# Two chained transformer blocks: block 1's first products are taken from the unnormalized x, and their results scaled by a row of inverse norms

## The reference, cut to what matters

```python
def rmsnorm(x, g):
    xf = x.astype(jnp.float32)
    y = xf * lax.rsqrt(jnp.mean(xf * xf, axis=-1, keepdims=True) + EPS)
    return (y * g.astype(jnp.float32)).astype(x.dtype)

def conformer_conv(u, b_glu, w_dw, b_dw, ln_g, ln_b):
    u = u + b_glu
    a, gate = jnp.split(u, 2, axis=-1)
    z = a * jax.nn.sigmoid(gate)
    ...          # causal depthwise convolution of 31 taps, layer norm, silu

def parallel_mixer(h, w_in, ...):        # h = rmsnorm(x, norm_mix_g)
    proj = h @ w_in
    q, k, v = ...                        # 512 columns each
    log_f = jax.nn.log_sigmoid(proj[..., OFF_F:OFF_C] + b_forget)
    attn = forgetting_attention(q, k, v, log_f)
    conv = conformer_conv(proj[..., OFF_C:], ...)
    return jnp.concatenate([attn, conv], axis=-1) @ w_out
```

## Time and profile before

| | us |
|---|---|
| median of the runs | 1259.65 |
| the profiled execution's own time | 1261.36 |
| its span, first to last instruction | 1259.5 |
| PE busy | 1097.0 (87%) |
| DVE busy | 624.7 (50%) |
| ACT busy | 437.5 (35%) |
| chain that ended last: PE / DMA / DVE / ACT | 58% / 32% / 6% / 2% |

### The profile page before, as it was taken

One profiled execution on the slowest core, in us unless ns is written; L12 is line 12 of the kernel. 1 busy time (PEld: TensorE's weight loads), 2 busy tenths in 40 slices (PEclk: granted clock), 3 DMA queues, 4 the chain that ended last, 5 costly groups with the idle time before them and its releaser, 6 DMA issues.

```text
span 1259.5 us, 17506 instructions
## 1 busy us (share of the span) xinstructions
PE 1097.0 (87%) x7555; PEld 792.5 (63%) x7555; DVE 624.7 (50%) x1005; ACT 437.5 (35%) x627; POOL 9.1 (1%) x19
## 2 busy tenths in 40 slices
PE   7999999998665666565768999999999999999997
PEld 6987898743121132121315988888886689998876
DVE  5998845620000000000004698986798766564465
ACT  4245434210000000000004566644586535544353
POOL 0000000000000000000000100000000000000000
PEclk9999999999798788898869999999999999999999
DMA  9543395699999999999999454554544064445430
GB/s 363 201 141 136 148 376 206 229 427 424 426 426 429 426 425 427 427 426 427 426 427 379 156 172 149 170 165 151 200 176 160 39 238 182 159 178 201 167 134 34
DMA packets 30031, 332.29 MB, mean 264 GB/s; under 512 B 3472, under 2 KB 3872, under 8 KB 5760
## 3 DMA queue, kind: packets, MB, share of 16 engines
q1 hardware_dynamic: 28928, 328.11, 66.0%
q0 software_dynamic: 1024, 3.02, 0.7%
HBM read 330.07 MB, written 1.05 MB: 263 GB/s over the span
## 4 chain that ended last, share of the span: by engine, by line
PE 58%; DMA 32%; DVE 6%; ACT 2%; issue 1%; SPq 0%; DVEq 0%; ACTq 0%
PE ps L632 13%; PE ps L649 11%; PE ps L709 10%; DMA arena<-in_w_up 10%; DMA arena<-in_w_down 7%; PE ps L1394 6%; DMA ring<-in_w_gate 4%; DMA arena<-in_w_gate 3%; DMA spare<-in_w_up 3%; DMA ring<-in_w_down 3%; PE ps L847 2%; PE ps L738 2%; PE ps L1026 2%; DMA ring<-in_units 1%; PE ps L761 1%; PE ps L584 1%
## 5 line engine op out<-in xcount | busy, mean ns | idle before, releaser
L1528 DVE TENSOR_TENSOR parts<-ring,parts 128x2048 fp32r<-128x2048 f32 x70 | 160.0, 2291 | 97.5 <-ACT parts L2377 97.0
L2377 ACT CAST parts<-ring 128x2048 fp32r<-128x2048 f32 x70 | 133.1, 1905 | 151.5 <-PE ps L632 66.8
L649 PE MATMUL ps<-parts 128*128 128x512 f32 x768 | 181.5, 394 | 0.9 <-DVE parts L1528 0.9
L1852 DVE TENSOR_TENSOR arena<-arena,ps 128x512 f32<-128x512 f32 x8 | 5.5, 687 | 340.0 <-PE ps L1026 340.0
L649 PEld LDWEIGHTS ps<-parts 128*128 128x128 f32 x768 | 143.1, 189 | 33.0 <-issue 2.8
L632 PE MATMUL ps<-parts 128*128 128x256 f32 x1344 | 163.2, 284 | 0.0
L632 PEld LDWEIGHTS ps<-parts 128*128 128x128 f32 x1344 | 161.9, 192 | 0.2
L709 PE MATMUL ps<-parts 128*128 128x512 f32 x576 | 137.2, 396 | 0.4 <-DVE parts L1697 0.4
L709 PEld LDWEIGHTS ps<-parts 128*128 128x128 f32 x576 | 108.0, 190 | 26.0 <-issue 3.0
L1026 PE MATMUL ps<-ring,arena 128*32 128x512 f32 x528 | 77.6, 721 | 41.8 <-DMA ring<-in_w_up 23.0
L1026 PE MATMUL ps<-arena 128*32 128x512 f32 x400 | 62.5, 760 | 36.2 <-DMA arena<-in_w_up 19.5
(11 more groups left out here) (373 smaller groups left out, 1336.4 us busy)
## 6 DMA issues: line engine op xcount, KB each, us to landing
ring<-in_units SPq DMA_DIRECT2D x35, 2048.0 KB, 8.2
ring<-in_w_gate SPq DMA_DIRECT2D x19, 2048.0 KB, 43.6
ring<-in_units SPq DMA_DIRECT2D x37, 1024.0 KB, 5.3
ring<-in_w_down SPq DMA_DIRECT2D x15, 2048.0 KB, 43.8
ring<-in_w_up SPq DMA_DIRECT2D x14, 2048.0 KB, 43.3
arena<-in_w_up SPq DMA_DIRECT2D x9, 2048.0 KB, 41.8
arena<-in_w_down SPq DMA_DIRECT2D x9, 2048.0 KB, 45.5
arena<-in_w_gate SPq DMA_DIRECT2D x6, 2048.0 KB, 43.5
```

Source lines behind the costliest of these rows:

```text
L649: mm = nc.tensor.matmul(banks[t], v[:, 4 * h + k, t * P:t * P + P], w[:, k, :], start=h + k + n == 0, stop=h == 1 and k == 3 and n == 2)
L1528: step(V.tensor_tensor(rest_half(name, h), split_half(name, h), w_high[stage][h].bitcast(F32), ALU.subtract), f"{stage}_rest_ready", wait= ...
L2377: step(S.copy(w_high[stage][h], split_half(name, h)), f"{stage}_high_ready", wait=False)
```

## The change

PE turns x itself, as soon as it and the identity matrix have landed. The sums of squares, the root and the reciprocal are taken meanwhile. DVE lays the inverse norms on the diagonals of two 128x128 matrices, and PE multiplies these by ones, which gives a row of inverse norms on every partition (`mix_row`). DVE scales by this row: the gates and the values of the convolution, the forget logits, and a whole copy of the turned x (`mix_x`), whose high part and rest then serve `q`, `k` and `v`. The memory's norm on DVE stands no longer ahead of the first gated channels but after the second. SP issues `q` ahead of `conv_a1`, and the memory behind `k`. Banks are dealt from bank 7 on, so that with the one more bank of `mix_row` all later ones get the numbers they had.

```diff
-        used, held, turn = [0] * BANKS, set(), [0]
+        used, held, turn = [0] * BANKS, set(), [7]
...
                 for t in range(TT):
-                    normed_half("mixT", t, t + 1)
-                idle_products(10)
+                    pe.wait_ge(sem(f"x_landed{t}"), 16)
+                    turn_half("mixT", x, t)
+                idle_products(6)
...
+                        if (c, name) == (0, "conv_g"):
+                            pe.wait_ge(sem("mixer_x_made"), 1)
+                            bank = open_bank("mix_row")
+                            for t in range(TT):
+                                mm = nc.tensor.matmul(bank[:, t * P:t * P + P], row_ones, row_diag[:, t * P:t * P + P], start=True, stop=True)
+                            close_bank(mm, "mix_row")
-                pe.wait_ge(sem("mixer_x_rest_ready"), 1)
+                pe.wait_ge(sem("mixer_x_made"), 3)
...
 (DVE)
+                step(V.memset(row_ones, 1.0), wait=False)
+                step(V.memset(z[:, :, 0:TAPS - 1], 0.0), wait=False)
+                step(V.memset(key_bias, 0.0), wait=False)
                 dve.wait_ge(sem("x_landed0"), 16)
-                normalize_half(x, normed, 4, 0)
+                step(V.tensor_tensor_reduce(normed[:, 0, :], x[:, 0, :], x[:, 0, :], 1.0, 0.0, ALU.mult, ALU.add, stat(4, 1)))
+                dve.wait_ge(sem("params_landed"), 16)
+                half_turned("mixT", xT, 0, "norm_mix_g")
+                half_turned("mixT", xT, 1, "norm_mix_g")
                 dve.wait_ge(sem("second_squared"), 1)
-                inverse_rms(stat(5, 1), stat(5, 1), D)
-                step(V.tensor_scalar(normed[:, 1, :], x[:, 1, :], stat(5, 1), None, ALU.mult), "x_normed")
+                inverse_rms(stat(4, 2), stat(4, 2), D)
+                step(V.tensor_scalar(row_diag[:, 0:P], ident, stat(4, 1), None, ALU.mult), wait=False)
+                step(V.tensor_scalar(row_diag[:, P:T], ident, stat(5, 1), None, ALU.mult), "mixer_x_made", wait=False)
...
+                bank = filled_by(dve, "mix_row")
+                drain(V.tensor_copy(mix_row, bank[:, 0:T]), "mix_row", wait=True)
+                def scale_gates(f):
+                    bank = filled_by(dve, f"conv_g{f}")
+                    ins = V.tensor_tensor(glu[:, 2 * f:2 * f + 2, :], grid(bank, 2), wide(mix_row.unsqueeze(1), [P, 2, T]), ALU.mult)
+                    drain(ins, f"conv_g{f}", wait=True)
+                scale_gates(0)
+                step(V.tensor_tensor(mix_x, xT, wide(mix_row.unsqueeze(1), [P, KT, T]), ALU.mult), "mixer_x_made", wait=False)
                 dve.wait_ge(sem("mixer_x_high_ready"), 1)
-                step(V.tensor_tensor(mix_rest, xT, mix_high.bitcast(F32), ALU.subtract), "mixer_x_rest_ready", wait=False)
-                dve.wait_ge(sem("mem_landed"), 16)
-                normalize(mem_tok, mem_normed, 0, "mem_normed")
+                step(V.tensor_tensor(mix_rest, mix_x, mix_high.bitcast(F32), ALU.subtract), "mixer_x_made", wait=False)
...
                 def gated_channels(f):
                     bank = filled_by(dve, f"conv_a{f}")
+                    ins = V.tensor_tensor(z[:, 2 * f:2 * f + 2, TAPS - 1:ZW], grid(bank, 2), wide(mix_row.unsqueeze(1), [P, 2, T]), ALU.mult)
+                    drain(ins, f"conv_a{f}", wait=True)
+                    dve.wait_ge(sem("gate_ready"), f + 1)
...
+                scale_gates(1)
                 convolve(range(1, 11), range(2))
                 gated_channels(1)
+                dve.wait_ge(sem("mem_landed"), 16)
+                normalize(mem_tok, mem_normed, 0, "mem_normed")
                 convolve(range(1, 8), range(2, 4))
                 split_rest("mixer", 1, 0)
...
 (ACT)
-                root()
+                act.wait_ge(sem("params_landed"), 16)
+                half_turned("mixT", xT, 0, "norm_mix_g")
                 act.wait_ge(sem("x_landed1"), 16)
                 step(S.activation(normed[:, 1, :], x[:, 1, :], ACT.Square, accum_out=stat(5, 1)), "second_squared", wait=False)
+                half_turned("mixT", xT, 1, "norm_mix_g")
                 root()
...
 (SP)
                 for c in range(2):
                     for name in BY_COLUMNS:
+                        if (c, name) == (1, "conv_a"):
+                            load(2)
                         load_columns(name, c)
-                sp.dma_start(mem_tok, d["mem"][0].rearrange("(t p) n -> p t n", p=P)).then_inc(sem("mem_landed"), 16)
-                for n in range(2, n_early):
+                for n in range(3, n_early):
                     load(n)
                     if n == 3:
+                        sp.dma_start(mem_tok, d["mem"][0].rearrange("(t p) n -> p t n", p=P)).then_inc(sem("mem_landed"), 16)
```

More of the change, by code:

```diff
@@ L322, in two_blocks_kernel @@
         mix_high, mix_rest = [grid(parts(n), KT) for n in (5, 1)]
+        mix_x = grid(page(1), KT)
+        row_ones, row_diag, mix_row = page(8, 1024, P), page(8, 1152, T), page(8, 1408, T)
         mem_high, mem_rest = [grid(parts_of_page[n][:, :], KT) for n in (8, 9)]
@@ L899, in _ @@
                 split_token_major("mem_kv3", "mem_v1", mem_high, mem_rest, turn_attention)
-                split_token_pair("out", {(1, 1): lambda: normed_half("normT", 0, 3)})
+                split_token_pair("out", {(1, 1): lambda: normed_half("normT", 0, 1)})
                 half_turned("normT", 0)
-                feature_pair(["mem_q0"], xT, lambda: normed_half("normT", 1, 4), lambda: half_turned("normT", 1))
+                feature_pair(["mem_q0"], xT, lambda: normed_half("normT", 1, 2), lambda: half_turned("normT", 1))
                 pe.wait_ge(sem("cross_x_rest_ready"), 1)
@@ L1568, in _ @@
-                dve.wait_ge(sem("mixer_x_high_ready"), 1)
-                step(V.tensor_tensor(mix_rest, xT, mix_high.bitcast(F32), ALU.subtract), "mixer_x_rest_ready", wait=False)
-                dve.wait_ge(sem("mem_landed"), 16)
-                normalize(mem_tok, mem_normed, 0, "mem_normed")
-                step(V.memset(z[:, :, 0:TAPS - 1], 0.0), wait=False)
-                step(V.memset(key_bias, 0.0))
+                inverse_rms(stat(4, 2), stat(4, 2), D)
+                dve.wait_ge(sem("ident_landed"), 16)
@@ L1578, in gated_channels @@
                     for cb in (2 * f, 2 * f + 1):
-                        ins = V.scalar_tensor_tensor(out=z[:, cb, TAPS - 1:ZW], in0=bank[:, (cb % 2) * T:(cb % 2) * T + T],
-                                                     scalar=col("b_glu", cb), in1=glu[:, cb, :], op0=ALU.add, op1=ALU.mult)
-                    drain(ins, f"conv_a{f}", wait=True)
+                        own = z[:, cb, TAPS - 1:ZW]
+                        step(V.scalar_tensor_tensor(out=own, in0=own, scalar=col("b_glu", cb), in1=glu[:, cb, :], op0=ALU.add, op1=ALU.mult),
+                             wait=cb % 2 == 1)
@@ L1613, in _ @@
                 tmp = page(4, 0, 1024)[0:HEADS, :].rearrange("p (n t) -> p n t", n=4)
-                drain(V.tensor_scalar(tmp[:, 0, :], bank[0:HEADS, 0:T], forget_b[:, 0:1], None, ALU.add), "forget", wait=True)
+                drain(V.tensor_tensor(tmp[:, 0, :], bank[0:HEADS, 0:T], mix_row[0:HEADS, :], ALU.mult), "forget", wait=True)
+                step(V.tensor_scalar(tmp[:, 0, :], tmp[:, 0, :], forget_b[:, 0:1], None, ALU.add))
                 step(V.tensor_scalar(tmp[:, 1, :], tmp[:, 0, :], -1.0, None, ALU.mult))
@@ L2077, in _ @@
                     rotate(k_rot, k_rot, NSA_KV)
-                step(V.memset(cmp_hid, 0.0), "cmp_hid_cleared")
+                step(V.memset(cmp_hid, 0.0), "cmp_cleared")
                 for h in range(2):
@@ L2112, in _ @@
                 filled_by(dve, "nq_rotT3")
-                step(V.memset(page(13, 1024, 1024), 0.0), "cmp_v_cleared", wait=False)
+                step(V.memset(page(13, 1024, 1024), 0.0), "cmp_cleared", wait=False)
                 step(V.memset(page(9, 0, 1024), 0.0), wait=False)
@@ L2393, in copy_out @@
                     drain(S.activation(dst, bank, func, scale=scale), fill)
-                root()
+                act.wait_ge(sem("params_landed"), 16)
+                half_turned("mixT", xT, 0, "norm_mix_g")
                 act.wait_ge(sem("x_landed1"), 16)
                 step(S.activation(normed[:, 1, :], x[:, 1, :], ACT.Square, accum_out=stat(5, 1)), "second_squared", wait=False)
+                half_turned("mixT", xT, 1, "norm_mix_g")
                 root()
[L2399 to L2403, removed]
                 def channel_gates(f):
-                    bank = filled_by(act, f"conv_g{f}")
+                    drained_by(act, f"conv_g{f}")
                     for cb in (2 * f, 2 * f + 1):
-                        ins = S.activation(glu[:, cb, :], bank[:, (cb % 2) * T:(cb % 2) * T + T], ACT.Sigmoid, bias=col("b_glu", 4 + cb))
-                    drain(ins, f"conv_g{f}")
+                        ins = S.activation(glu[:, cb, :], glu[:, cb, :], ACT.Sigmoid, bias=col("b_glu", 4 + cb))
```

(9 more changed lines are left out.)

9 lines of the change are left out of this document (3 added, 6 removed).

## The result

The changed kernel takes 1268.88 us (median of four runs, 1266.82 to 1269.97) against 1259.68 (1259.02 to 1260.97): 1.0065 times as long, interval 1.005 to 1.0081. Forecast were 1268.5. The profiled execution took 1268.83 us, with a span of 1267.1 (1259.5 before). Three executions further down, of 1435.87, 1586.5 and (kernel before) 1585.68 us, ran at mean granted clocks of 0.74, 0.65 and 0.65, and all medians and ratios here leave them out.

A forecast was written before the change was run, and what follows sets the result against it. PE alone was taken to bound the old chain from 7.42 to 62.7 us. Start 0.4, mix_row 0.45, wait for k's rest 5.9 and clock 2.1 gave 8.85, so 1259.65 + 8.85 = 1268.5 us; range 1264.5 to 1272.

The forecast's parts named there:

- The wait in front of k: PE, between q and k: DVE has the first rest of k at 57.8, PE wants it at 52.0; 5.9 us.
- The clock behind it: PE at k's start: slow clock after standing still for 5.9 us; 2.1 us lost, with 0 and 2.7 as ends.
- mix_row: PE, ahead of q: two added full products of 128 columns on its path, 0.22 us each, 0.45 together.
- The start: PE's first full unit at about 12.3 instead of 11.88, behind ACT's table load and copies; 0.4 us later.
- The slow first unit: Rival: PE starts conv_g0 at 1.2 GHz after a short wait, some 2 us lost, 1270.5 us; chance 0.15.
- What follows: After block 1's start, through the experts: PE leads, no later cover, so its shift counts at full size, 8.8 us.
- Loads and bank numbers: Earlier q, later conv_a1 and memory, new bank numbers and a joined semaphore: claimed to cost nothing.

The follow-up runs named there:

- a variant: Changed kernel with one small activation ahead of everything on ACT, so that its table is loaded at the start; 1268.36 us, ratio 1.0056.
- Filling the gap: Changed kernel with 44 idle products on PE between q and k, timed twice; 1268.2 us (ratio 1.007) and 1266.16 us (1.0058).
- both repeats: The changed kernel timed and profiled again twice, unchanged; 1268.69 and 1268.2 us, ratio 1.0068 each against the kernel before.
- the four variants without a gap there: Changed kernel with 20 idle products instead of 6 (1267.76 us), table load plus 44 idle products (1265.8), early table load alone (1268.36), or four cures together (1259.9).
- the second repeat: The changed kernel, unchanged, as yardstick of a later group and third look at its first unit; 1268.2 us, ratio 1.0068.

## Why the prediction was right

The path was right: the written order of DVE's line, with the memory's norm in it, makes PE wait in front of `k`, and the slow clock follows. The total lies within half a microsecond of the forecast of 1268.5 partly by luck: a term of 1.9 us that I had left out of the sum was made up for by one that was too large and by what got lost on the way to the end.

**The wait in front of k** was forecast at 5.9 us and measured at 5.87, 5.81 and 5.81. Its working held link by link: 7.7 us from `mix_row` to the first gated channels (21.24 to 28.89, 7.65), 30.3 from there to the rest (28.89 to 59.16, 30.27). Both ends came 1.4 us later than written, with the slow first unit in front of them. Moving the norm (4.7 us) in either kernel, either way, made and unmade the wait as the sum says: 4.7 less of it in the changed kernel, 2.99 us where there had been none in the old one.

**The clock behind it:** 2.1 forecast; 1.9, 1.9 and 1.7 measured in the three profiles of the changed kernel, and 0.2 of restart; 2.5 in a variant. Filling the gap took the clock's part away.

**mix_row:** 0.45 and 0.46.

**The start** was mis-sized: 12.3 forecast, 11.92 measured, +0.04 for +0.4. Two things were off by little: the identity matrix landed 0.1 us earlier and PE began at 6.01, and I had laid ACT's steps end to end, while the square begins 1.02 us behind the start of four copies that are written down with 1.14. That the load stands behind the bank, the step that undid the 1.2 us of earlier transposes, was right (7.21), and taking it away gave 1.3 us.

**The slow first unit** was a rival with a chance of 0.15, and it came true in all three profiles of the changed kernel: 1.9 us. I weighed it by a gap of 1.61 us in the experts that left the clock up. PE here had only just begun to work, and slowly: its 16 transposes took 3.4 to 3.7 us, where 32 took 3.84 at 2.4 GHz. That this is the difference is argued and not shown, since the same start also gave fast units. With this term the kernel should have been at 1259.65 + 10.2, near 1270; the runs say 1268.9. So the total was hit with a term too few in it, and about one microsecond that did not arrive.

**What follows:** that the shift goes on whole is right up to the experts (10.2 at 240 us, 10.6 at 299). At the end it is between 7.6 and 8.7 us in three profiles (spans of 1267.1, 1268.2 and 1267.9 against 1259.5). Of the first pair's difference 1.7 us is the clock in the second block; the rest goes in small steps, half a microsecond in the experts (9.7 behind the last of them, 10.0 in both repeats) and 0.7 up to 965 us (1.1 and 1.5 in the repeats). What takes it up there is not shown.

**Loads and bank numbers** cost nothing, as said.

## What to carry to other kernels

Before work is taken off the front of a chain, write the line of the engine that does the new work up to its next deadline: here DVE had 1.4 us of cover, and by my count 8.1 us were put against it. Idle time of an engine is worth something only to instructions that the written order lets stand in it; the same norm was free at 14 us and cost nearly 7 at 46. And a wait put on the matrix engine is to be priced with the slow clock behind it: waits of 3.0 to 5.9 us brought 1.5 to 2.5 us more here, one of 1.13 us brought none.

## What the runs showed that I had not expected

- The first unit of seven profiles with six idle products and ACT's load in the way took 8.83, 8.83, 8.91 and 8.92 us in four and 7.14 in three (the norm moved early, and both with the filled gap), and the edit of the last two acts only long after 12 us. The length of the gap ahead of the unit doesn't sort them: 1.90, 1.88, 0.97 and 0.96 us where the unit took 8.8 to 8.9, and 0.97, 0.96 and 1.00 where it took 7.14. In the four variants without a gap there the unit took 7.07, 7.10, 7.20 and 7.68 us. What decides it stays open.
- In two of those that took 8.9 us the granted clock reads 1.00 from 12.4 to 14 us, where PE began five rows in 1.6 us, as in a profile that reads 0.50 there; the variants at full speed began nine or ten. The row is that of the second repeat. Near the start, durations are to be trusted before the recorded clock.

```profile
12.40:14.00 1.60, 1.60 (x5) 1.33 (x4) 0.72 (x4) 1.57 (x3) 0.00 (x0) 1.00 1.13 481
```

- A gap of 1.13 us in front of `k` left the granted clock at 1.00 (2.4 GHz); one of 2.99 us already cost 1.5 us, close to the 1.7 to 1.9 of one twice as long. Where such a gap cost 2.5 us, the granted clock stood at 0.50 for 5.7 us behind it and not for 4.
